# A gated conv/mLSTM layer: a guard computed in squares, an earlier table load, and one wait moved in the tail

## The reference

```
s   = einsum('bthk,bshk->btsh', qc, kc) * w_intra
num = einsum('btsh,bshv->bthv', s, vc) + w_inter * einsum('bhvk,bthk->bthv', C, qc)
den = sum(s, axis=2) + w_inter * einsum('bhk,bthk->bth', n, qc)
h   = num / maximum(abs(den), exp(-m_t))
hm  = hm * rsqrt(mean(hm * hm, axis=-1) + EPS) * g_mh
hm  = hm * sigmoid(o)
```

## Time and profile before

| what | us |
|---|---|
| timed runs, median (lowest to highest) | 1263.68 (1263.58 to 1264.84) |
| the profiled execution's own time | 1266.74 |
| its span in the trace | 1265.2 |
| TensorE busy | 1243.7 (98%) |
| VectorE busy | 716.6 (57%) |
| ScalarE busy | 497.5 (39%) |
| mean granted clock of TensorE | 0.995 of full speed |

### The profile page before, as it was taken

The page is one execution under the profiler, slowest core; times in us unless marked ns, Lnnn a source line. Parts: engine busy times, 40 slices in busy tenths (PEclk is TensorE's granted clock), DMA queues, the critical chain, the costliest instruction groups (busy, mean ns, idle before and its releaser), DMA issues.

```text
span 1265.2 us, 23540 instructions
## 1 busy us (share of the span) xinstructions
PE 1243.7 (98%) x9041; PEld 1167.8 (92%) x9041; DVE 716.6 (57%) x1009; ACT 497.5 (39%) x751; POOL 62.1 (5%) x127
## 2 busy tenths in 40 slices
PE   8999999999999999999999999998999999999998
PEld 7999968888797888879999999997999999999998
DVE  6342687888778888878455434337444122443334
ACT  5333443353354344435553222235554223544221
POOL 4010001101100110110000000000000000000000
PEclk9999999999999999999999999998999999999999
DMA  6235216515451651532322232331322222223212
GB/s 204 81 119 184 92 49 218 196 46 175 157 176 47 218 207 35 196 138 84 99 85 84 83 100 80 140 99 34 101 99 85 99 83 83 84 83 100 83 67 71
DMA packets 40355, 141.20 MB, mean 112 GB/s; under 512 B 4804, under 2 KB 7236, under 8 KB 40184
## 3 DMA queue, kind: packets, MB, share of 16 engines
q1 hardware_dynamic: 28888, 99.37, 23.6%
q0 software_dynamic: 11424, 41.23, 9.3%
HBM read 118.31 MB, written 22.26 MB: 111 GB/s over the span
## 4 chain that ended last, share of the span: by engine, by line
PE 92%; ACT 3%; DVE 2%; DMA 2%; issue 1%; DVEq 0%; SPq 0%; ACTq 0%
PE product L1451 86%; PE side L1451 6%; DMA wraw<-in_wstream 1%; ACT whi L554 1%; DMA x<-in_xT 1%; DVE accp L1076 0%; DVE wlo L913 0%; ACT sqh L749 0%; DVE crg L1197 0%; PE side L1609 0%; ACT L716 0%; DVE hm L1220 0%; DVE sqacc L1223 0%; ACT hm L720 0%; ACT sqacc L715 0%
## 5 line engine op out<-in xcount | busy, mean ns | idle before, releaser
L913 DVE TENSOR_TENSOR wlo<-wraw,whi 128x1024 fp32r<-128x1024 f32 x176 | 215.3, 1224 | 231.9 <-ACT whi L554 227.8
L1451 PE MATMUL product<-ahi,whi 128*128 128x256 f32 x1520 | 319.7, 292 | 10.1 <-DVE alo L1335 5.9
L1451 PE MATMUL product<-ahi,wlo 128*128 128x256 f32 x1520 | 316.4, 289 | 0.0
L1451 PE MATMUL product<-alo,whi 128*128 128x256 f32 x1520 | 315.8, 289 | 0.0
L554 ACT ACTIVATE whi<-wraw 128x1024 fp32r<-128x1024 f32 x176 | 184.4, 1052 | 228.1 <-PE product L1451 185.0
L1451 PEld LDWEIGHTS product<-ahi,whi 128*128 128x128 f32 x1520 | 248.0, 190 | 18.4 <-issue 12.1
L1451 PEld LDWEIGHTS product<-alo,whi 128*128 128x128 f32 x1520 | 247.3, 191 | 0.0
L1451 PEld LDWEIGHTS product<-ahi,wlo 128*128 128x128 f32 x1520 | 245.7, 189 | 0.0
L1076 DVE SCALAR_TENSOR_TENSOR accp<-u,wdw,accp 128x512 f32<-128x512 f32 x240 | 163.4, 745 | 0.3
L1451 PE MATMUL product<-hidhi,whi 128*128 128x288 f32 (+1 forms) x512 | 111.0, 288 | 1.0 <-issue 1.0
L1451 PE MATMUL product<-hidhi,wlo 128*128 128x288 f32 (+1 forms) x512 | 111.0, 288 | 0.0
(11 more groups left out here) (290 smaller groups left out, 1617.8 us busy)
## 6 DMA issues: line engine op xcount, KB each, us to landing
wraw<-in_wstream SPq DMA_DIRECT2D x176, 512.0 KB, 3.4
crg<-in_c_in POOLq DMA_DIRECT2D x32, 512.0 KB, 6.4
out_c_s<-crg POOLq DMA_DIRECT2D x32, 512.0 KB, 2.9
hb<-head_rows POOLq DMA_DIRECT2D x4, 580.0 KB, 5.4
x<-in_xT SPq DMA_DIRECT2D x4, 544.0 KB, 5.5
sgm<-in_xT SPq DMA_DIRECT2D x1, 2176.0 KB, 8.8
out_c_p<-cst POOLq DMA_DIRECT2D x4, 512.0 KB, 8.0
out_yT<-y SPq DMA_DIRECT2D x4, 288.0 KB, 2.3
```

What stands on the lines that cost most here:

```text
L913: V.tensor_tensor(wlo[:, k % RING, :, :], wraw[:, k % 2, :, :], whi[:, k % RING, :, :].bitcast(f32), ALU.subtract).then_inc(lo_done, 1)
L1451: return pe.matmul(out, lhsT, rhs, start=start, stop=stop, skip_group_check=check)
```

## The change

- ScalarE writes the scaled square of den straight into `sqacc` (one Square in place of the Abs). The row of exp(-m) is now exp(-2m + ln(share)), with the logarithm as a bias from a new constant `ln_share`, which GpSimd sets with one more memset. VectorE takes `min` with a cap and `max` with `sqacc` in one operation. The second Square and the buffer `rden` are gone.
- On ScalarE the dummy sigmoid stands right behind that Square, the rounding of chunk 10 behind it, and the rounding of chunk 11 behind the sigmoid of `o0`.
- On VectorE the remainder of chunk 10 goes behind update(0), update(1) ahead of chunk 11, and update(2) and update(3) ahead of chunk 12. `O_TAPS` changes from 0, 3, 5, 2 taps to 2, 0, 6, 2.
- In the tail the wait for accumulator 1 goes behind the two half products that write accumulator 0.

```diff
-O_TAPS = [(14, 14), (14, 17), (17, 22), (22, 24)]
+O_TAPS = [(14, 16), (16, 16), (16, 22), (22, 24)]
-D_CAP = 1e18
+SHARE = EPS * DV / P
+CAP = SHARE * 1e36
...
+            pool.memset(ln_share[:, :], math.log(SHARE)).then_inc(pool_step, 1)
...
-                act.activation(hb[:, R_M:R_M + SEQ], hb[:, R_M:R_M + SEQ], ACT.Exp, scale=-1.0).then_inc(expm_ready, 1)
+                act.activation(hb[:, R_M:R_M + SEQ], hb[:, R_M:R_M + SEQ], ACT.Exp, bias=ln_share[:, :], scale=-2.0).then_inc(expm_ready, 1)
...
                 act.wait_ge(den_ready, h + 1)
-                act.activation(rden[:, :], side[:, 0, :], ACT.Abs).then_inc(den_abs, 1)
+                act.activation(sqacc[:, :], side[:, 0, :], ACT.Square, scale=SHARE ** 0.5).then_inc(den_squared, 1)
+                act.activation(warm[:, :], eps[:, :], ACT.Sigmoid).then_inc(table_in, 1)
                 split(10)
-                act.wait_ge(d_ready, h + 1)
-                act.activation(sqacc[:, :], rden[:, :], ACT.Square, scale=(EPS * DV / P) ** 0.5).then_inc(hsq_ready, 1)
-                act.activation(warm[:, :], eps[:, :], ACT.Sigmoid).then_inc(table_in, 1)
                 for k in range(VT):
-                    split(11 + k)
+                    if k > 0:
+                        split(11 + k)
                     s = use(f"o{k}")
                     act.activation(tile(hm, 4 * h + k), slot(s), ACT.Sigmoid, bias=c("b_o", 4 * h + k)).then_inc(drained[s], 1)
+                    if k == 0:
+                        split(11)
...
-                dve.wait_ge(den_abs, h + 1)
+                dve.wait_ge(den_squared, h + 1)
                 dve.wait_ge(expm_ready, h + 1)
-                V.scalar_tensor_tensor(rden[:, :], hb[:, R_M:R_M + SEQ], D_CAP, rden[:, :], ALU.min, ALU.max).then_inc(d_ready, 1)
-                split(10)
+                V.scalar_tensor_tensor(sqacc[:, :], hb[:, R_M:R_M + SEQ], CAP, sqacc[:, :], ALU.min, ALU.max).then_inc(d_ready, 1)
...
                     if k == 0:
                         update(0)
+                        split(10)
+                        update(1)
+                    if k == 1:
+                        update(2)
+                        update(3)
                     split(11 + k)
                     taps(*O_TAPS[k])
-                    if k == 1:
-                        update(2)
-                    if k < 2:
-                        update(2 * k + 1)
...
-                    dve.wait_ge(hsq_ready, (VT + 1) * h + (k + 2))
+                    dve.wait_ge(hsq_ready, VT * h + (k + 1))
...
                     if k >= 1:
                         dve.wait_ge(hsum_ready, VT * h + k)
+                    else:
+                        dve.wait_ge(d_ready, h + 1)
...
-                pe.wait_ge(den_abs, h + 1)
+                pe.wait_ge(den_squared, h + 1)
...
-            for s in range(2):
-                free(s, KT // 2 - 1 + sf + HID // 2)
             for k in range(4):
+                if k % 2 == 0:
+                    free(k // 2, KT // 2 - 1 + sf + HID // 2)
                 half_product(0, k)
```

More of the change, by code:

```diff
@@ L8 @@
+import math
 import concourse.bass as bass
@@ L161, in hybrid_layer @@
         tiny = at("tiny", [P, 1], f32)
+        ln_share = at("ln_share", [P, 1], f32)
         warm = at("warm", [P, 1], f32)
@@ L209, in hybrid_layer @@
         sqacc = at("sqacc", [P, SEQ], f32)
-        rden = at("rden", [P, SEQ], f32)
         qm = at("qm", [P, QT, DEC_B * NS], f32)
@@ L296, in hybrid_layer @@
             "expm_ready", "wkp_ready", "vs_hi", "vs_all", "kh_ready", "ops_ready"))
-        den_ready, den_abs, sden_ready, sden_abs = sem("den_ready"), sem("den_abs"), sem("sden_ready"), sem("sden_abs")
+        den_ready, den_squared, sden_ready, sden_abs = sem("den_ready"), sem("den_squared"), sem("sden_ready"), sem("sden_abs")
         srec_ready, conv_sum, conv_copied = sem("srec_ready"), sem("conv_sum"), sem("conv_copied")
@@ L456, in _ @@
             pool.memset(tiny[:, :], 1e-36).then_inc(pool_step, 1)
+            pool.memset(ln_share[:, :], math.log(SHARE)).then_inc(pool_step, 1)
             for j in range(QUAD):
-                pool.wait_ge(pool_step, 19 + j)
+                pool.wait_ge(pool_step, 20 + j)
                 pool.affine_select(out=sel[:, :], in_=sel[:, :], compare_op=ALU.not_equal, fill=1.0, base=-NS * j,
@@ L646, in _ @@
             act.wait_ge(const_in, 32)
-            act.wait_ge(pool_step, 23)
+            act.wait_ge(pool_step, 24)
             with act.Fori(0, HEADS) as h:
@@ L1050, in _ @@
             dve.wait_ge(drained[1], KT)
-            dve.wait_ge(pool_step, 23)
+            dve.wait_ge(pool_step, 24)
             with dve.Fori(0, HEADS) as h:
@@ L1547, in _ @@
             pe.wait_ge(asmp_ready, 2)
-            pe.wait_ge(pool_step, 23)
+            pe.wait_ge(pool_step, 24)
             with pe.Fori(0, HEADS) as h:
```

## The result

The changed kernel takes 1256.89 us (median of five runs, 1256.55 to 1258.22), the kernel before 1263.7: a ratio of 0.9946, interval 0.9932 to 0.996. A repetition gave 1257.31 (0.9948, 0.9935 to 0.9962). The sign was right, 6.8 us came where 5.2 were forecast, and the range's low end, 1257.2, was missed by 0.3. The parts of the sum were further off than the sum: a term that I did not have brought 4.3, the clock's 1.53 was not there, and the state loads cost some 1.2 for my 0.2. That the sum came so near is luck: these errors have opposite signs. The profiled execution took 1258.22, with a span of 1256.7 (before 1266.74 and 1265.2).

What follows compares the result with a forecast made beforehand. The prediction took TensorE to bound the kernel (86% `product`, 6% `side` of the span). Its terms, 1.53 + 1.53 + 0.78 + 0.33 + 1.25 - 0.2 = 5.2, off the median 1263.68 gave 1258.5 us, range 1257.2 to 1262.4.

Steps and rivals of the forecast that it cites:

- What bounds the kernel: Whole run: TensorE ends last; only its standing still or a low clock leaves time to gain.
- Pool.: Very start, GpSimd: one memset of 128x1 and a wait for 24 instead of 23; nothing, at most 0.1.
- The clock, 1.53: Turn 0, behind the 1.40 us gap: the low clock's cost comes back, 1.53 us; bounds 0 and 1.53.
- My first rival: Turn 0: the clock term is not there, as timed runs had no fall or it comes anyway; 1260.0, chance 0.18.
- my weighing of a rule: Clock in turn 0: such a gap may or may not bring a fall; the sum would then be 3.7, not 5.2.
- `o1` in turn 0, 1.53: Turn 0: outer(1)'s wait for the sigmoid goes and `o1` starts at 188.40, not 190.04; 1.53 us, bounds 1.2 to 1.7.
- Turns 1 to 3, 0.78: Head loop, turns 1 to 3: `o1` starts earlier, right behind update(0); 0.78 us gained, bounds 0.5 and 1.5.
- `o2`, 0.33: Turns 1 to 3: with four taps ahead of update(2), `o2` starts without a fill; 0.11 in each, 0.33 us.
- VectorE: Head loop: 2.6 us moved between update(3) and update(4) costs nothing; 0.6 idle is left ahead of update(4).
- The state loads, 0.2: Head loop, readout(1): chunk 14's later weight load shares queues with state transfers; 0.2 us lost.
- The tail, 1.25: Tail: first half product at 1228.46 instead of 1229.62, and the fill goes; 1.25 us, bounds 1.0 and 1.3.
- The rival on the slower side: Head loop: late state loads make readout(1) wait about 1.40 and the clock fall each turn; 6.3 slower, 1270.0, chance 0.05.

Runs made afterwards that it cites:

- pad32: The kernel before with only 32 unused bytes where the change puts `ln_share`: 1259.76 us, 0.9967.
- after_dveold: The changed kernel with VectorE's order of before, all else changed: 1266.14 us, 1.001.
- both_off: The kernel before with 32 unused bytes ahead of the weight tiles and 32 more ahead of the moving tiles: 1264.61 us in its one run.
- experiment 5: The changed kernel repeated (1257.31 us), with VectorE's old order (1266.14), and with the remainder of chunk 12 and its taps ahead of update(2) (1272.17).
- all64: The kernel before with 64 unused bytes ahead of all tiles: 1262.81 us.
- tail_only: The kernel before with only the tail's wait moved: 1262.61 us, 0.9988.
- head_off: The changed kernel with the tail's wait as before and 32 unused bytes more, thus without the change's layout: 1265.22 us, 1.001.
- after_off: The changed kernel with 32 unused bytes more, so that `ahi` is again 32 off a 64-byte boundary: 1263.49 us, 0.9995.
- experiment 4: The kernel before with only the tail's wait moved (1262.61 us); the changed kernel with the tail's wait as before and 32 unused bytes (1265.22).

## Why the prediction was right and where it was wrong

**What bounds the kernel: right.** Each us gained is TensorE's: standing still, at the low clock, or, what I had not thought of, running at another pace. I wrote that "only two things can shorten the run"; there is a third, and that sentence is the error.

**The step that failed: a term of 4.3 us put at nothing.** "*Pool.* One memset of 128x1 ... so nothing; at most 0.1" prices `ln_share` as an instruction. It is also an allocation, and its 32 bytes moved the activations to the weights' place modulo 64; `pad32`, which has nothing but these bytes, gains 4.3. Without this term the time would have lain well inside the range. The trace of before hardly says so: its matmuls' 125.56 ns look like the pace of the engine, and only its second feed-forward product, 12.00 a pair beside 12.05 elsewhere, shows that there is another.

**The clock, 1.53: the price right, the term not in the median.** A fall costs what I said, 1.5 in before and 1.5 to 1.6 in `after_dveold` (2.6 in `both_off`), and it stands with a gap. But in turn 0 only two of the eight executions with the old order have it, and the profiled execution of before was one. It took 3.1 more than the median, and I took 1.53 off a median in which few runs, if any, can have had it. Of 30 timed runs of before, 24 took 1262.75 to 1265.1 and six 1265.92 to 1267.1; by its time the profiled one is of the six, but their mean clock is no lower than that of the others, so what makes those six longer is not shown. My first rival said just this, and so did my weighing of a rule. The Trainium skill ("TensorE: Matmul & The Clock Gate", Part 1) has the clock set by a monitor that runs freely, not in step with the kernel. These runs agree: in turn 0 gaps of 1.30 to 1.34 brought no fall and one of 1.40 did, and in experiment 5 one of 0.87 brought a fall and one of 1.93 none.

**`o1` in turn 0, 1.53: right.** All of it went as written: `hm` at 186.97 (it ends at 187.68 where I had said ahead of 187.4, but outer(0) too began 0.23 later), outer(1) at 188.23 (near 188.1), the table load hidden, the wait gone. Outer(0) to outer(1) went from 3.09 to 1.61. In the other seven executions with the old order it was 1.78 in `all64`, 2.55 and 2.61 in `tail_only` and `pad32`, 2.98 to 3.01 in three and 3.63 in `both_off`: the gap hangs on when chunk 10's weights land. The gain is thus between 0.2 and 2.0, and 1.4 in the middle of the eight.

**Turns 1 to 3, 0.78: high by 0.2.** 1.81, 1.86 and 1.75 became 1.61, 1.62 and 1.62: 0.57.

**`o2`, 0.33: right.** Outer(3) to `side<-kw,vtok` took 12.72, 12.66 and 12.77 in turns 1 to 3 and takes 12.54: 0.53 in all. The layout gives 0.08 of each (two chunks), which leaves 0.29.

**VectorE: right, for too small a reason.** update(4) had 0.65 of idle time left where I had 0.6. But I priced the new order as a cost of nothing and a gain of 0.33; experiment 5 shows that it carries the head's whole edit: without it the change would be 9 us slower than it is. I had the table load hidden by chunk 10's DMA, which holds in turn 0 alone, where that DMA was 1.57 late; in the other turns it was 0.23 to 0.34 late, and in turn 1 the load puts chunk 10 back by 1.2. The new order on VectorE is what makes that harmless.

**The state loads, 0.2: too low.** Measured 1.7 in one execution and 0.7 in the next (0.9 in `head_off`, 0.5 in `after_off`). The reasoning was right, more transfers about save 3. I bounded it by turn 0's slack, 0.9, but the changed kernel waited in turns 1 and 2, and the longest wait was in turn 2 each time. And the "0 to 0.5 a turn" for the sigmoid of `o1` behind chunk 12's rounding came at 0.24 in turn 1 (outer(2) to outer(3) 1.91 for 1.67), and not in the repetition.

**The tail, 1.25: right.** 1.4 and 1.7 in the two timed pairs, the gap gone.

**The sum again.** 5.2 less 1.53 for the clock, less 0.1 for turn 0, less 0.2 for turns 1 to 3, less 1.0 for the state loads (1.2, the mean of the two, for 0.2) is 2.4; with the layout 6.7. Measured 6.8 (6.9 in the repetition). Of the 2.4, 1.25 are the tail's and about 1.1 the head's, which is what experiment 4 has.

The rival on the slower side did not come: the state loads were late by at most 1.13 and the clock held behind them. Its threshold, a wait as long as turn 0's 1.40, had no ground: experiment 5 has falls behind 0.87 and 0.98.

Not settled: why TensorE's pace hangs on the distance of the tiles; when a gap brings a fall; and the entry to the feed-forward part. There TensorE stands for 5.93 us before and 5.94 after. Before, the clock is at full speed until near the gap's end and then low while TensorE works, from 863.6 to about 869.5; after, it falls inside the gap and is low only from 859.0 to about 862. From the end of the long stage to the next long piece it is 34.70 to 36.22 us in the sixteen profiled executions, whatever their edit; after has the shortest and before the longest. This makes 1.5 of the 8.5 between the two spans, and nothing says that it is part of the change.

## What to carry to other kernels

An added tile is a change of every address behind it: before pricing a change, compare where the operands of the hot matmuls lie, modulo 64 and 128 bytes, and try the kernel before with unused bytes in their place. Each part of the change is then compared with a kernel of its own layout. A kernel that is bound by TensorE may owe something to the distance of its tiles, which no wait, gap or clock of its profile shows, only the mean time of a matmul next to another layout's. A gap and a fall of clock in one profiled execution are no term of a median until they are seen again. When one engine's work is brought forward, the order of the engine that feeds the next step must be brought forward with it.

## What the runs showed of the hardware that I had not expected

- fp32r matmuls of 256 and 288 columns: 124.78 ns in the mean where moving and stationary tile lie equal modulo 64 bytes, 125.56 where they lie 32 apart, 0.6%. In the product whose moving operand alternates between two tiles, two chunks take 12.00 us with these at distances of 0 and 64 or of 96 and 32 modulo 128, 12.13 at 32 and 96, 12.10 at 0 and 96.
- Weight transfers of 512 KB landed in 3.4 us in the median of all, and needed 7.0 beside state loads and saves. Chunk 10's in turn 0 was from 0.26 to 2.08 late for ScalarE in eight kernels that do not differ ahead of it but in unused bytes.
- The clock fell with gaps of 0.87, 0.98, 1.01, 1.70, 1.92 and 2.44 us in experiment 5 and of 1.40 and 1.95 in turn 0, and did not with 0.97 and 1.93 in experiment 5 and 0.87, 0.93, 1.30, 1.33 and 1.34 in turn 0. A fall with a gap of about 1 us cost 1.5 to 1.6.
